# Input chunks in front of the rotary angles, and half a unit in front of the recurrence's norm sum

## The reference

```python
def apply_rope(t, cos, sin):
    t1, t2 = jnp.split(t, 2, axis=-1)
    return jnp.concatenate([t1 * cos - t2 * sin, t1 * sin + t2 * cos], axis=-1)

# first block, layer 0: h = x
a = rms_norm(h, norm_gains[0, 0]); proj = a @ w_in        # c_q 512, c_kv 256, k_r 64
k_rope = apply_rope(k_r, cos, sin)                        # angles: positions * inv_freq

# first block, layer 1: the recurrence, for each head
f = lb + (1 - lb) * sigmoid(f_x); k = 1 - f; b = cumsum(log f) within a chunk of 32
q_rel = q * exp(b - b_ref); k_rel = k * exp(b_ref - b)
q_dec = q * exp(b);         k_dec = k * exp(b_last - b)
o_intra = where(causal, q_rel @ k_rel.T, 0) @ v
o_inter = q_dec @ state;    state = dec * state + k_dec.T @ v      # 16 chunks in a row
o = rms_norm(o_intra + o_inter, o_norm) * silu(g)
```

## Time and profile before

| | |
|---|---|
| median of three runs | 2646.51 us (2645.14 to 2648.08) |
| the profiled execution | 2645.55 us, its span 2643.7 us |
| busy in the span | PE 97%, PEld 79%, POOL 73%, DVE 42%, ACT 25% |
| chain that ended last | PE 90%, DVE 6%, ACT 1%, issue 1% |
| mean granted clock of TensorE | 0.994 of full |

### The profile page before, as it was taken

The page is one execution under the profiler, slowest core; times in us unless marked ns, Lnnn a source line. Parts: engine busy times, 40 slices in busy tenths (PEclk is TensorE's granted clock), DMA queues, the critical chain, the costliest instruction groups (busy, mean ns, idle before and its releaser), DMA issues.

```text
span 2643.7 us, 32593 instructions
## 1 busy us (share of the span) xinstructions
PE 2568.2 (97%) x11823; PEld 2087.8 (79%) x11823; DVE 1103.6 (42%) x1907; ACT 662.7 (25%) x1110; POOL 1940.3 (73%) x1664
## 2 busy tenths in 40 slices
PE   6999999998999899999998999999999999999999
PEld 5777888887788688888776888888877877888887
DVE  6543311126777432112587352525441332643433
ACT  2443210014444321001356221203112022421111
POOL 5455888886666588888580888887967856888784
PEclk9999999999999999999999999999999999999999
DMA  5122233232222223333210233332212212333231
GB/s 155 53 72 64 83 105 99 95 95 64 80 63 80 64 80 96 97 99 98 72 55 26 80 96 96 96 96 94 98 64 95 79 63 80 96 96 100 92 108 68
DMA packets 285701, 224.26 MB, mean 85 GB/s; under 512 B 13363, under 2 KB 278556, under 8 KB 285468
## 3 DMA queue, kind: packets, MB, share of 16 engines
q1 hardware_dynamic: 285020, 222.44, 27.4%
q10 hardware_dynamic: 576, 0.40, 0.1%
HBM read 220.72 MB, written 2.10 MB: 84 GB/s over the span
## 4 chain that ended last, share of the span: by engine, by line
PE 90%; DVE 6%; issue 1%; ACT 1%; DVEq 1%; DMA 0%; POOL 0%; ACTq 0%
PE proj L611 26%; PE proj L613 26%; PE proj L612 26%; PE aux L2199 1%; DVE top L1753 1%; DVEq L1756 1%; PE proj L636 1%; PE proj L641 1%; PE proj L637 1%; PE aux L2003 1%; PE aux L2173 1%; PE aux L840 1%; PE proj L781 1%; PE aux L459 0%; DVE F L805 0%
## 5 line engine op out<-in xcount | busy, mean ns | idle before, releaser
L611 PE MATMUL proj<-a_hi,w_hi 128*128 128x512 f32 x1992 | 795.3, 399 | 1.4 <-DVE a_lo L810 1.4
L613 PE MATMUL proj<-a_hi,w_lo 128*128 128x512 f32 x1992 | 776.8, 390 | 0.0
L612 PE MATMUL proj<-a_lo,w_hi 128*128 128x512 f32 x1992 | 776.2, 390 | 0.0
L1230 POOL TENSOR_TENSOR w_hi<-raw,small 128x512 fp32r<-128x512 f32 x373 | 394.0, 1056 | 443.9 <-PE proj L613 345.9
L1237 POOL TENSOR_TENSOR w_hi<-raw,small 128x512 fp32r<-128x512 f32 (+2 forms) x449 | 487.2, 1085 | 192.4 <-PE proj L613 192.3
L1242 POOL TENSOR_TENSOR w_lo<-raw,w_hi 128x512 fp32r<-128x512 f32 (+2 forms) x449 | 593.2, 1321 | 6.0
L1241 POOL TENSOR_TENSOR w_lo<-raw,w_hi 128x512 fp32r<-128x512 f32 x372 | 484.5, 1302 | 29.2
L611 PE MATMUL proj<-g_hi,w_hi 128*128 128x512 f32 x1200 | 470.0, 392 | 3.7 <-DVE a_lo L810 1.4
L613 PE MATMUL proj<-g_hi,w_lo 128*128 128x512 f32 x1200 | 467.0, 389 | 0.0
L612 PE MATMUL proj<-g_lo,w_hi 128*128 128x512 f32 x1200 | 466.9, 389 | 0.0
L611 PEld LDWEIGHTS proj<-a_hi,w_hi 128*128 128x128 f32 x1992 | 374.7, 188 | 84.5 <-issue 5.3
(11 more groups left out here) (289 smaller groups left out, 2295.9 us busy)
## 6 DMA issues: line engine op xcount, KB each, us to landing
raw<-in_mlp_w SPq DMA_DIRECT2D x64, 1024.0 KB, 5.3
raw<-in_f_w_up SPq DMA_DIRECT2D x88, 512.0 KB, 4.8
raw<-in_b_w_in SPq DMA_DIRECT2D x24, 1024.0 KB, 5.1
raw<-in_hgrn_w_in SPq DMA_DIRECT2D x32, 512.0 KB, 4.9
raw<-in_f_w_down SPq DMA_DIRECT2D x16, 1024.0 KB, 4.9
raw<-in_b_w_out SPq DMA_DIRECT2D x8, 1024.0 KB, 5.0
raw<-in_f_w_down SPq DMA_DIRECT2D x8, 768.0 KB, 4.3
raw<-in_a_w_in SPq DMA_DIRECT2D x5, 1024.0 KB, 5.3
```

Of the source, the lines that this page charges most:

```text
L611: pe.matmul(psum[r][:], w_hi[r][:, w], xh, start=k == 0, stop=False)
L612: pe.matmul(psum[r][:], w_hi[r][:, w], xl, start=False, stop=False)
L613: last = pe.matmul(psum[r][:], w_lo[r][:, w], xh, start=False, stop=k == kc - 1)
L1230: first = pool.tensor_tensor(hi[:, 0:n], src[:, 0:n], nothing.to_broadcast([P, n, P]), ALU.subtract)
```

## The change

Three parts. First, DVE takes the input's chunks behind five angle instructions; the other seven, and the sine's sign, come later, behind the first two takes and in front of the rotation. ACT's sines move behind its first two squares, with a reload of the table for logarithm and exponential behind them. Second, SP issues the row loads in front of slab 2 as before, but the table loads in front of slab 3. Third, in the recurrence the first half of unit 1 (4 of 8 chunks) stands in front of the sum, behind unit 0; the second half stays in front of the outer products. In head 0, where unit 2 was cut in half around scores and keys, the cuts are now at chunks 5 and 6.

```diff
-            def small_loads():
+            def row_parts():
                 for dst, src in row_loads:
                     sp.dma_start(dst, src).then_inc(rows_in, 16)
+
+            def late_tables():
                 for k in TABLE_WIDTH:
...
                         if st.slab_base + q == 2:
-                            small_loads()
+                            row_parts()
+                        if st.slab_base + q == 3:
+                            late_tables()
...
-            sine(0, rope_sin, reduced)
-            sine(1, rope_cos, reduced_cos)
...
             square_c(0)
             square_c(1)
+            sine(0, rope_sin, reduced)
+            sine(1, rope_cos, reduced_cos)
+            log_and_exp(act)
             act.wait_ge(*setup_lb_diff)
...
             step(dve.tensor_scalar(cycles, cycles, -ROUND, None, ALU.add))
-            for n, part in enumerate(TWO_PI):
-                step(dve.scalar_tensor_tensor(reduced, cycles, -part, reduced if n else angle, ALU.mult, ALU.add))
...
             take_c(0)
             take_c(1)
-            dve.wait_ge(*sin_ready.at(1))
-            step(dve.tensor_scalar(rope_sin, rope_sin, rope_sign, None, ALU.mult))
+            for n, part in enumerate(TWO_PI):
+                step(dve.scalar_tensor_tensor(reduced, cycles, -part, reduced if n else angle, ALU.mult, ALU.add))
...
+            dve.wait_ge(*sin_ready.at(1))
+            step(dve.tensor_scalar(rope_sin, rope_sin, rope_sign, None, ALU.mult))
             rotate(st_mla_in, KR_UNIT, k_rope, k_rope_turned)
...
+            HG_EARLY = DC // 2
+
+            def hg_chunks(j, i, ks):
+                if ks.start == 0:
+                    open_unit(pe, st_hg, j, i)
+                for k in ks:
+                    unit_chunk(pe, st_hg, j, k, DC, a_hi, a_lo)
+
...
-            open_unit(pe, st_hg, 2, 1)
-            for k in range(DC // 2):
-                unit_chunk(pe, st_hg, 2, k, DC, a_hi, a_lo)
+            hg_chunks(2, 1, range(DC - 3))
             hg_inside(0)
+            hg_chunks(2, 1, range(DC - 3, DC - 2))
             hg_keys(0)
-            for k in range(DC // 2, DC):
-                unit_chunk(pe, st_hg, 2, k, DC, a_hi, a_lo)
+            hg_chunks(2, 1, range(DC - 2, DC))
             hg_outer(0)
             hg_units((3,), 1)
             hg_output(0)
             hg_units((0,), 2)
+            hg_chunks(1, 2, range(HG_EARLY))

             def hg_head(i):
                 n_hg.sum(pe, 0, 0, i - 1)
                 hg_inside(i)
                 hg_keys(i)
-                hg_units((1,), i + 1)
+                hg_chunks(1, i + 1, range(HG_EARLY, DC))
                 hg_outer(i)
                 hg_units((2, 3), i + 1)
                 hg_output(i)
             with pe.Fori(1, HG_HEADS - 2) as i:
                 hg_head(i)
                 hg_units((0,), i + 2)
+                hg_chunks(1, i + 2, range(HG_EARLY))
             hg_head(HG_HEADS - 2)
```

More of the change, by code:

```diff
@@ L1537, in _ @@
             take_c(1)
-            dve.wait_ge(*sin_ready.at(1))
-            step(dve.tensor_scalar(rope_sin, rope_sin, rope_sign, None, ALU.mult))
+            for n, part in enumerate(TWO_PI):
+                step(dve.scalar_tensor_tensor(reduced, cycles, -part, reduced if n else angle, ALU.mult, ALU.add))
+            dve.tensor_scalar(reduced, reduced, 3.1415925, -3.1415925, ALU.min, ALU.max).then_inc(angle_ready.sem, 1)
+            dve.wait_ge(*angle_ready.at(0))
+            step(dve.tensor_scalar(cycles, reduced, np.pi / 2, -2 * np.pi, ALU.is_gt, ALU.mult))
+            step(dve.scalar_tensor_tensor(reduced_cos, cycles, np.pi / 2, reduced, ALU.add, ALU.add))
+            dve.tensor_scalar(reduced_cos, reduced_cos, 3.1415925, -3.1415925, ALU.min, ALU.max).then_inc(angle_ready.sem, 1)
             z = [lb[:, k * DC:k * DC + DC] for k in range(8)]
```

## The result

The changed kernel is slower: 2662.67 us, the median of five runs (2660.15 to 2665.28), against 2646.23 us for the kernel before on the same chip (median of five). The ratio estimated from the runs is 1.0055, with a 95% interval of 1.0044 to 1.0066; the quotient of the two medians, 1.0062, lies in it. The medians differ by +16.4 us where +11.2 was forecast. The profiled execution took 2665.28 us (span 2663.5); it is the slowest of the five, so its difference to the profile of before is +19.8 us of span, about 3 us more than the medians differ by.

What follows compares the result with a forecast made beforehand. TensorE works almost throughout, so time moves only where it idles or runs at half clock. Terms -6.9 - 1.1 + 0 + 12.8 + 6.4 = +11.2 us gave a median of 2657.7 us, range 2649.5 to 2662.5.

Steps and rivals of the forecast that it cites:

- The start, -6.9: Input chunks taken 8.22 us earlier, less a 1.28 us table load on the path: first projection at 22.1, -6.9 us.
- The moved angle work, cost 0: Seven angle instructions (8.2 us) between DVE's second and third take, hidden by 2 us of slack before the sums: 0.
- The tables on SP, cost 0: Third weight load issued earlier, table loads behind it; nobody on the path waits for either: 0.
- Head 0, -1.1: Recurrence, head 0: wait before the keys shrinks from 1.53 to 0.17; outer products at 656.36, not 657.48: -1.1 us.
- Head 1, 0: Recurrence, head 1: old waits of 1.81 and 0.88 go, a new one of some 2.6 comes: 0, between -0.3 and +0.3.
- Heads 2 to 6, 5 x 2.55: Recurrence: outer products wait 2.55 us per head for ACT's copy of the turned keys: +12.8 us.
- The clock, four falls of six: Half clock behind four of the six new waits in the recurrence, 1.6 us each: +6.4 us; bounds 0 and 9.6.
- No fall of the clock: Rival: the same new waits in the recurrence, but full clock throughout: +4.8, 2651.3 us; chance 0.15.
- The faster rival: Outer products don't wait for the chain behind the sum, or it shrinks below 5.5 us: -11.0, 2635.5 us; chance 0.08.
- the point of decision: Recurrence: 5.5 us from the sum to the copied keys, below which the half unit only covers waits.
- The lost start: Rival: moved angle work comes too late, so the start gives nothing: up to 6.9 us more, 2664.6 us; chance 0.07.

Runs made afterwards that it cites:

- front_only: The changed kernel with TensorE's order in the recurrence put back as before: 2641.0 us, ratio 0.9977 to the kernel before.
- tables_only: The kernel before with only SP's part of the change, the eight table loads behind the third weight load: 2647.87 us, ratio 1.0001.
- filled: The changed kernel with ten added matmuls of 512 columns in front of the outer products of heads 1 to 6: 2655.22 us, ratio 1.0026 to before.
- short_chain: The changed kernel with ACT's copies of turned values and keys right behind the norm's exponential, DVE's masked scores ahead of the gating: 2637.85 us, ratio 0.9961 to before.
- rec_only: The kernel before with only the recurrence's new order: 2667.06 us, ratio 1.0071.

## Why the prediction was right, and where it was off

The forecast held in sign, in mechanism and in place; 2662.67 lies 5.0 us above the 2657.7 forecast and 0.2 above the upper end of the range, 2662.5. As a ratio to before that end is 1.0060 (2662.5 / 2646.51), and 1.0055 was measured: the time is at the range's edge. By its steps:

- **The start, -6.9.** Right: -6.8 in `front_only`. a_hi was due at 14.57 and came at 14.12, with the data 0.5 earlier. The Trainium skill's drain of 1.38 us (ScalarE: Activation LUTs, What ACT_TABLE_LOAD costs) would have given 5.6: here the load of 12.82 ends at 14.10, the activation behind it starts at 14.12, and the gain was the one without a drain. So the measurement decides against that sentence for this place.
- **The moved angle work, cost 0.** The outcome was right, its size was not: seven instructions took 9.9 us (38.53 to 48.45) and not 8.2; the first three alone 4.45, where they took 2.86 at their old place, since there GpSimd began its first split only at 13.22, and here it worked beside all three. The third take came at 50.63 and not 49.8, and the slack shrank from 2 us to 1.3. It still covered.
- **The tables on SP, cost 0.** Right, by `tables_only`.
- **Head 0, -1.1.** Right. The outer products stood at 657.48 and stand at 651.09, 6.4 us earlier, where the matmuls in front of the head stood 5.3 earlier; the other kernels with this order gained 1.1 there too. The keys' wait shrank from 1.53 to 0.37 and not 0.17, and 0.22 us lie in front of the outer products without a cause that the profile shows.
- **Head 1, 0.** Wrong by +1.15: I said that both old waits go. The sum's went, but TensorE waited 1.76 us for the keys. DVE's work for them ended at 674.63, 4.8 earlier than before, where TensorE had come 5.7 earlier. Two of its operations had got slower beside GpSimd, L1635 and L1641, 1.60 and 1.35 us where both took 0.69 before. DVE's scaling of the norm stands behind that work in its order and so began at 674.54 only; the chain from the sum to the outer products was 9.8 us (670.59 to 680.38) and not 8.1 to 8.7. I had let DVE keep its pace while TensorE's order changed; GpSimd's splits moved with TensorE.
- **Heads 2 to 6, 5 x 2.55.** Right: 5 x 2.49. That it is the chain behind the sum, and that the sum starts it, is shown from two sides: `filled` (2.43 us of added work, no change of distance) and `short_chain` (distance 5.48, no wait).
- **The clock, four falls of six.** This is a term that was mis-sized: five of six in the heads at 1.6 us (34.16 to 34.22 from one head's outer products to the next, against 30.08 + 2.49), 8.0 us. The size of one fall was right; four was a choice between bounds and no reading. The 3.0 us at 891.7 aren't part of this term, since kernels with the old order have half clock there too. `rec_only` fell six times in six, and `filled`, with no wait to speak of, nowhere in the heads. That it goes with the idle stretches is shown by `filled`; why the clock fell in head 1 of `rec_only` behind 1.88 us and not in the kernel after behind 2.22 is open.
- **The rivals.** "No fall of the clock" would have given 2651.3; the filled kernel shows what it looks like, 2655.2. The faster rival is out: the distance stayed 8.05 us, not under 5.5. It comes true in `short_chain`, where the point of decision was crossed: its -11.0 stands against -10.0 there. The lost start is out.

The forecast sum of +11.2 against the medians' +16.4: 1.6 for the fifth fall and 1.15 for head 1, less 0.3 for the shorter waits, make 2.5. The rest, 2.8, isn't traced to a step of the change. Stretches of half clock outside the heads (at 246, 605 and 891.7 us, 0.8 to 3.0 us each in the profiled pair) came and went from one profile to the next whatever the kernel, and may hold it; no run separates that.

## What to carry to other kernels

Moving work in front of a step helps the step that waits for something earlier, and takes the same work from behind it: ask which chain starts at the step itself, and compare its length with what stays behind. Here 8.1 us of chain met 8.2 us of work, a balance with no slack, and 2.7 us of it were moved away. Before the matmuls are moved, look at the order of the other engines: an operation with no need of the slow part (ACT's copies) stood behind it. With TensorE's new order two edits there turned +16.4 us into -10.0; with its old order the same two gave about 1 us, so their worth is that they take away a loss which the new order had made. A short wait repeated in each pass may cost a stretch of half clock besides itself: 2.49 us idle plus 1.6 us. And before a stretch of half clock is put down to a change, look whether it is there in a second profile of the old kernel.

## What the runs showed of the hardware that was not expected

- The granted clock fell behind 2.48 to 2.50 us of idle TensorE five times in five (heads 2 to 6) and not behind 2.22 us, while in `rec_only` it fell behind 1.88 us and five times behind 2.37 to 2.38. It did not fall behind waits of 1.2 us in either kernel with fewer chunks in front.
- DVE's operations with two inputs of 128x512 in SBUF (TENSOR_TENSOR F<-F) took 0.68 us free and 1.35 to 1.79 beside GpSimd's, while one that reads a bank (F<-proj,F, at 663.83 in the kernel after) took 0.68 beside it too; three scalar-tensor ones took 4.45 us beside it, against 2.86 at their old place. Which operations are hit changes with TensorE's order, since GpSimd's splits follow the end of a unit.
- The activation behind a table load started 0.02 us after the load's end.
